# Choosing the engine of squares, sums, residual adds and norm-weight products one by one while a schedule is built

## The reference, cut to what matters

```python
for layer in range(2):
    xn = rmsnorm(h, mix_norm_g[layer])            # h * rsqrt(mean(h*h)) * g
    if layer == 0:                                # 1024 -> 2048 columns
        mix = concat(pool_mixer(a), gate_b * short_conv(gate_c * xb)) @ ab_w_out
    else:                                         # 1024 -> 2560 columns
        uv = gelu(p[..., :1024]); u, v = split(uv)
        c_out = u * (W_s @ layernorm(v) + b)      # in chunks of 128 positions
        # attention of 8 heads: weight = sigmoid(z_ts) * prod_{s<j<t} (1 - sigmoid(z_tj))
        d_out = stick_breaking_attention(q, k, v)
        mix = concat(c_out, d_out) @ cd_w_out
    h = h + mix
    hn = rmsnorm(h, mlp_norm_g[layer])
    h = h + square(relu(hn @ mlp_w1[layer])) @ mlp_w2[layer]      # 1024 -> 4096 -> 1024
return rmsnorm(h, final_norm_g)
```

## Time and profile before

| what | value |
|---|---|
| median of three runs | 2921.53 us (2921.23 to 2926.58) |
| the profiled execution | 2921.85 us |
| its span on the slowest core (core 5) | 2920.1 us; the eight cores 2896.3 to 2920.1 |
| mean granted TensorE clock on core 5 | 0.983 |
| PE, PEld | 2797.7 us (96%), 1194.9 us (41%) |
| DVE, ACT, POOL | 1436.4 (49%), 1261.6 (43%), 1602.0 us (55%) |

### The profile page before, as it was taken

One profiled execution on the slowest core, in us unless ns is written; L12 is line 12 of the kernel. 1 busy time (PEld: TensorE's weight loads), 2 busy tenths in 40 slices (PEclk: granted clock), 3 DMA queues, 4 the chain that ended last, 5 costly groups with the idle time before them and its releaser, 6 DMA issues.

```text
span 2920.1 us, 43942 instructions; the slowest of 8 cores (2896.3 to 2920.1 us)
## 1 busy us (share of the span) xinstructions
PE 2797.7 (96%) x13211; PEld 1194.9 (41%) x13211; DVE 1436.4 (49%) x1759; ACT 1261.6 (43%) x2062; POOL 1602.0 (55%) x1793
## 2 busy tenths in 40 slices
PE   8999999999999999799998999999999989999998
PEld 3444444444443344343443444444444434444443
DVE  4411246464435555776645454445565675554003
ACT  3433234736335344365543353433645464444231
POOL 4655515765417777576761465550576766674333
PEclk9999999999999999899999999999999999999999
DMA  8798883456665999746755344465355485446222
GB/s 171 157 208 196 177 216 90 120 150 147 184 155 107 193 177 175 190 123 157 167 139 155 85 107 113 114 157 170 92 123 123 106 216 135 114 114 184 86 77 83
DMA packets 491478, 420.24 MB, mean 144 GB/s; under 512 B 310128, under 2 KB 334960, under 8 KB 491248
## 3 DMA queue, kind: packets, MB, share of 16 engines
q1 hardware_dynamic: 465184, 370.07, 49.1%
q0 software_dynamic: 26064, 47.36, 11.3%
HBM read 304.23 MB, written 89.13 MB: 135 GB/s over the span
## 4 chain that ended last, share of the span: by engine, by line
PE 79%; DMA 6%; DVE 6%; issue 4%; POOL 3%; ACT 2%; SPq 1%; DVEq 0%; POOLq 0%; ACTq 0%
PE ps L588 74%; PE ps L1349 3%; PE ps L1402 2%; DMA stg<-xT 2%; DMA ring<-wblk 1%; DVE vt L1209 1%; DVE P L1365 1%; DMA h<-xT 1%; POOL Wq L1379 1%; DMA Wk<-Wq 1%; SPq L581 1%; DVE X L746 1%; POOL ps L1064 1%; DMA ring<-wbf 1%; POOL ffB L937 0%
## 5 line engine op out<-in xcount | busy, mean ns | idle before, releaser
L588 PE MATMUL ps<-X,ring 128*128 128x512 bf16 x6144 | 1399.1, 383 | 36.3 <-DVE X L746 11.1
L588 PEld LDWEIGHTS ps<-X,ring 128*128 128x128 bf16 x6144 | 586.0, 98 | 778.9 <-issue 121.5
L1379 POOL TENSOR_TENSOR Wq<-P 128x1024 bf16<-128x1024 f32 (+2 forms) x320 | 529.1, 1655 | 299.3 <-DVE P L1365 289.7
L588 PE MATMUL ps<-mix,ring 128*128 128x512 bf16 x2816 | 657.0, 380 | 7.2 <-POOL P L1360 4.1
L1365 DVE TENSOR_TENSOR_SCAN P<-ps,carry,cbs 128x512 f32<-128x512 f32 x384 | 488.9, 1279 | 346.1 <-POOL P L1360 200.6
L578 ACT ACTIVATE ps<-ps 128x512 f32<-128x512 f32 (+3 forms) x576 | 429.6, 750 | 477.4 <-PE ps L588 238.2
L588 PE MATMUL ps<-ffB,ring 128*128 128x512 bf16 x2048 | 485.1, 380 | 0.0
L811 DVE TENSOR_TENSOR tmp<-ps,ms 128x512 f32<-128x512 f32 x256 | 175.3, 685 | 494.0 <-PE ps L588 493.3
L816 POOL TENSOR_TENSOR h<-tmp,h 128x512 f32<-128x512 f32 x224 | 287.7, 1284 | 229.9 <-DVE tmp L811 229.1
L588 PEld LDWEIGHTS ps<-mix,ring 128*128 128x128 bf16 x2816 | 263.8, 98 | 339.7 <-issue 39.6
L1365 DVE TENSOR_TENSOR_SCAN P<-ps,cbs 128x128 f32<-128x128 f32 (+3 forms) x256 | 208.1, 819 | 323.6 <-ACT ps L578 189.4
(11 more groups left out here) (82 smaller groups left out, 1755.2 us busy)
## 6 DMA issues: line engine op xcount, KB each, us to landing
ring<-wbf SPq DMA_DIRECT2D x540, 256.0 KB, 3.0
ring<-wblk POOLq DMA_DIRECT2D x180, 256.0 KB, 7.9
wbf<-ring SPq DMA_DIRECT2D x180, 256.0 KB, 6.4
stg<-xT SPq DMA_DIRECT2D x96, 256.0 KB, 4.8
h<-xT SPq DMA_DIRECT2D x64, 256.0 KB, 7.4
hsp<-h SPq DMA_DIRECT2D x64, 256.0 KB, 3.7
h<-hsp SPq DMA_DIRECT2D x64, 256.0 KB, 6.2
oT<-mixf SPq DMA_DIRECT2D x32, 256.0 KB, 5.1
```

What stands on the lines that cost most here:

```text
L588: ins = pe.matmul(out, lhsT=l, rhs=r, start=(first and i == 0), stop=(last and i == n - 1), skip_group_check=True)
L1379: yield Req("pool", lambda e: e.tensor_tensor(out=W4, in0=P[:, :, 1:w + 1].rearrange("p h (j n) -> p h j n", n=128), in1=P[:, :, 0:w].rear ...
```

## The change

Three things change. First, a `Req` may carry alternatives: `Machine.run` works out, for each, planned start plus duration plus a cost, and books the one that comes out least. Squares, sums of squares, residual adds and products with the norm weights get alternatives on POOL, ACT or DVE; a MLP tile now always gets a Relu into tmp, and its square any of three engines. Second, planned numbers are replaced, with a price of 1.28 us for a change of ACT's function table. Third, an S stage's out_proj takes the scratch at t = 0, not at t = 1.

```diff
-DMA_KB_US = 256.0
+DMA_KB_US = 230.0
...
+        if r.tab is not None and r.tab != self.tab:
+            self.tab = r.tab
+            start += 1.28
...
                     st = S.ready(r)
+                    if r.alts:
+                        k0 = st + r.dur + r.cost
+                        for q in f.req.alts:
+                            s1 = S.ready(q)
+                            if s1 + q.dur + q.cost < k0:
+                                k0, r, st = s1 + q.dur + q.cost, q, s1
...
+    def any_of(self, *reqs):
+        reqs[0].alts = reqs[1:]
+        return reqs[0]
+
+    def sq_any(self, out, in_, reads, writes, dve=False, bias=0.0):
+
+        p = Req("pool", lambda e: e.tensor_tensor(out=out, in0=in_, in1=in_, op=ALU.mult), reads, writes, 1.06, bias=bias)
+        d = Req("dve", lambda e: e.tensor_tensor(out=out, in0=in_, in1=in_, op=ALU.mult), reads, writes, 0.70, bias=bias)
+        d.cost = 1.5
+        a = Req("act", lambda e: e.activation(out=out, in_=in_, func=AF.Square), reads, writes, 0.63, bias=bias)
+        return self.any_of(p, a, d) if dve else self.any_of(p, a)
...
-        if x == 2 and not odd:
-            yield Req("pool", lambda e: e.tensor_tensor(out=Xf[:, SQ[i][odd], hs], in0=sq, in1=sq, op=ALU.mult), Ls,
-                          [LX[k][t] for k in rows[odd]], 1.15, bias=0.5)
+        if x:
+            yield self.sq_any(Xf[:, SQ[i][odd], hs], sq, Ls, Lw)
...
+            yield self.any_of(add("pool", 1.29, 0.0), add("dve", 0.72, 0.3 if x == 1 and i == 3 or eng == "dve" else 1.5))
...
-            if c % 2:
-                yield Req("dve", lambda e: e.tensor_scalar(out=X[:, c, ts], in0=self.h[:, c, ts], scalar1=g, scalar2=None,
-                                                           op0=ALU.mult),
-                          [self.Lh[c][t], self.Lcf], [LX[c][t]], 0.50)
-            else:
-                yield Req("act", lambda e: e.activation(out=X[:, c, ts], in_=self.h[:, c, ts], func=AF.Copy, scale=g),
-                          [self.Lh[c][t], self.Lcf], [LX[c][t]], 0.72)
+            d = Req("dve", lambda e: e.tensor_scalar(out=X[:, c, ts], in0=self.h[:, c, ts], scalar1=g, scalar2=None,
+                                                     op0=ALU.mult),
+                    [self.Lh[c][t], self.Lcf], [LX[c][t]], 0.55)
+            d.cost = 0.2
+            yield self.any_of(d, Req("act", lambda e: e.activation(out=X[:, c, ts], in_=self.h[:, c, ts], func=AF.Copy, scale=g),
+                                     [self.Lh[c][t], self.Lcf], [LX[c][t]], 0.72))
...
+            yield self.any_of(add("pool", 1.29, 0.0), add("dve", 0.71, 0.2 if last and c >= 6 else 1.5))
...
-                if (j + t) % 2:
-                    b = yield self.p_tmp
-                    m = self.tmp[:, b, :]
-                    yield self.act(m, ap, AF.Relu, [], [self.Lbank[bk], self.Ltmp[b]], TT, True)
-                    self.banks.free(bk)
-                    yield Req("pool", lambda e: e.tensor_tensor(out=F[:, jj, ts], in0=m, in1=m, op=ALU.mult),
-                              [self.Ltmp[b]], [LF[jj][t]], 1.15)
-                    self.p_tmp.free(b)
-                else:
-                    yield self.act(ap, ap, AF.Relu, [], [self.Lbank[bk]], TT, True)
-                    yield self.act(F[:, jj, ts], ap, AF.Square, [], [self.Lbank[bk], LF[jj][t]], TT, True)
-                    self.banks.free(bk)
+                b = yield self.p_tmp
+                m = self.tmp[:, b, :]
+                yield self.act(m, ap, AF.Relu, [], [self.Lbank[bk], self.Ltmp[b]], TT, True)
+                self.banks.free(bk)
+                yield self.sq_any(F[:, jj, ts], m, [self.Ltmp[b]], [LF[jj][t]], True)
+                self.p_tmp.free(b)
...
-            if t == 1:
-                yield lambda: not self.finbusy
+            if t == 1 or kind == "S":
+                yield lambda: not self.finbusy or kind == "S" and t == 0
                 self.use_scratch("ff")
...
-        yield Req("pe", zmm, [self.LqT[a][tq], self.LkT[a][c]], Lz, w / 2400.0 + 0.07, bias=-0.04, wslack=0.5)
+        yield Req("pe", zmm, [self.LqT[a][tq], self.LkT[a][c]], Lz, w / 2400.0 + 0.37, bias=-0.04, wslack=0.5)
...
-                  [LWq], [LWk[r]], 1.25, key=("wk", k, r), lat=4.0, kb=w * 0.69)
+                  [LWq], [LWk[r]], 1.22, key=("wk", k, r), lat=1.6, kb=w * 0.4)
...
-                      0.15 + 0.216 * (2.5 if first else 4), bias=-0.04, slack=4.0)
+                      0.45 + 0.216 * (2.5 if first else 4), bias=-0.04, slack=4.0)
```

More of the change, by code:

```diff
@@ L197 @@
 class Req:
-    __slots__ = ("eng", "fn", "reads", "writes", "key", "dur", "lat", "bias", "kb", "slack", "wslack")
+    __slots__ = ("eng", "fn", "reads", "writes", "key", "dur", "lat", "bias", "kb", "slack", "wslack", "alts", "cost", "tab")
     def __init__(self, eng, fn, reads, writes, dur, key=None, lat=0.0, bias=0.0, kb=256.0, slack=0.0, wslack=0.0):
@@ L211, in __init__ @@
         self.wslack = wslack
+        self.alts = ()
+        self.cost = 0.0
+        self.tab = None
 class Pool:
@@ L698, in square, with add @@
             yield lambda: c - 1 in ev.done
-            if i == 3 and x == 1:
-                eng = "dve"
-            yield Req(eng, lambda e: e.tensor_tensor(
-                out=X[:, SQ[i][2], t * TT:(t + 1) * TT].rearrange("p (a n) -> p a n", a=2),
-                in0=Xf[:, SQ[i][0], hs], in1=Xf[:, SQ[i][1], hs], op=ALU.add),
-                [LX[k][t] for k in rows[1]], [LX[k][t] for k in rows[0]], 0.70 if eng == "dve" else 1.15)
+            def add(eng, d, cost):
+                q = Req(eng, lambda e: e.tensor_tensor(
+                    out=X[:, SQ[i][2], t * TT:(t + 1) * TT].rearrange("p (a n) -> p a n", a=2),
+                    in0=Xf[:, SQ[i][0], hs], in1=Xf[:, SQ[i][1], hs], op=ALU.add),
+                    [LX[k][t] for k in rows[1]], [LX[k][t] for k in rows[0]], d)
+                q.cost = cost
+                return q
+            yield self.any_of(add("pool", 1.29, 0.0), add("dve", 0.72, 0.3 if x == 1 and i == 3 or eng == "dve" else 1.5))
             ev.sums.add(i)
@@ L814, in evac, with add @@
             self.banks.free(bk)
-            eng, d = ("dve", 0.70) if last and c >= 6 else ("pool", 1.15)
-            yield Req(eng, lambda e: e.tensor_tensor(out=self.h[:, c, ts], in0=self.tmp[:, b, :], in1=self.h[:, c, ts],
-                                                     op=ALU.add),
-                      [self.Ltmp[b]], [self.Lh[c][t]], d)
+            def add(eng, d, cost):
+                q = Req(eng, lambda e: e.tensor_tensor(out=self.h[:, c, ts], in0=self.tmp[:, b, :], in1=self.h[:, c, ts],
+                                                       op=ALU.add),
+                        [self.Ltmp[b]], [self.Lh[c][t]], d)
+                q.cost = cost
+                return q
+            yield self.any_of(add("pool", 1.29, 0.0), add("dve", 0.71, 0.2 if last and c >= 6 else 1.5))
             self.p_tmp.free(b)
```

29 lines of the change are left out of this document (17 added, 12 removed).

## The result

The kernel after takes 2959.34 us (median of four runs, 2954.13 to 2964.15); the ratio to the runs of before is 1.0126, 95% interval 1.0105 to 1.0147. It is slower by 1.3%; forecast were 2914.5 us and a range to 2934. For the kernel after it is +39 us, against the 2908.4 to 2909.2 us of the runs of before in the experiments; against the one profiled run of before that was measured with it, it is 36.

A forecast was written before the change was run, and what follows sets the result against it. PE was taken as the bound, busy 2797.7 of 2920.1 us. Terms -7 - 3 + 1.5 + 1 + 1.5 - 1 = -7.0 gave 2914.8 for the profiled run, 2914.5 for the median; range 2896 to 2934.

The forecast's parts named there:

- part 2: F00's W2: new DMA figures spread the x products and remove an old PE wait; -3 us, bounds -5.4 and +8.
- part 5: AV matmuls nearer to their last scores, median distance 88 to 64 matmuls, may wait for transposes; +1.5 us, bounds 0 to +13.
- late transposes: Second form of slower: AV waits in S00 at their upper bound, 2928.5 us; chance 0.07 together with F00.
- Part 1: End of S00's out_proj: PE's 6.23 us wait for POOL's last sum and slow clock behind it shrink; -7.0 us.
- Part 3: Out_projs: 63 more norm-weight products on DVE at 0.835 us overfill it; +1.5 us, bounds 0 to +15; adds cost nothing.
- 0.49 us for a product beside an idle POOL: DVE norm-weight product when POOL is idle; if all 63 were so, their term would be about +0.5 instead of +1.5.
- The 1.26 us product of the earlier trace: A DVE norm-weight product beside POOL, said to end where a POOL sum ends, taken as agreeing with shared SBUF interfaces.
- Part 4: W1 beside attention: MLP squares on ACT add 3.7 us per 20, making 20.8 and 21.6; +1 us, bounds 0 to +5.
- the rival on it: Slower: ACT bounds W1 under attention in six stages; +9.5 us, 2931 us, chance 0.18.
- the 10 that were to show an ACT at its limit: Sign of a wrong forecast: PE waits on ACT ps, ACT tmp or ACT ffB of 10 us and more.
- Part 6: S00's late score: a 4.6 us wait shortens because a POOL square before the scan leaves; -1 us, bounds 0 to -6.
- What stays: Norm chains ending in DVE X, 29.8 us of PE waits, held as long after the change, since all links stay.

The follow-up runs named there:

- e10: Kernel after with only the scores' and AV's planned durations of before, the transposes' new landing kept: ratio 1.0025, +6.8 us.
- e1: Kernel before with one edit, every MLP tile's Relu into tmp and its square on ACT: ratio 0.9988, -4.8 us.
- e9: Kernel after with only the transposes' planned numbers of before, the scores' and AV's longer durations kept: ratio 1.0116, +38.7 us.
- e6: Kernel after with attention's planned numbers of before (scores, AV and transposes): ratio 1.0022, +5.3 us.
- e4: Kernel after with the planned numbers of before and the scratch at t = 1, engine choices kept: ratio 1.0004, -0.2 us.
- e13: Kernel before with a matmul of 512 columns planned at 0.2257 us instead of 0.2157: one run, 2929.1 us, +10.3 us.
- e14: Kernel after with the planned matmul at 0.2057 us instead of 0.2157: ratio 1.0056, +21.2 us.
- e17: Kernel before with attention's new planned numbers and the planned matmul at 0.2057 us: ratio 1.0061, +22.1 us.
- e5: Kernel after with an S stage's out_proj taking the scratch at t = 1 again: ratio 1.0147, two runs, +33 us.
- e7: Kernel after with the planned DMA rate (256) and kept blocks' size (150) of before: ratio 1.0089, +27 us.
- e8: Kernel after without a price for ACT's table switch, Ln 1.3 and Exp 0.9 as before: ratio 1.0091, +30 us.

## Why the prediction was wrong

The step that failed is the list of parts itself. From the new planned numbers the prediction took the DMA figures (part 2) and the transposes' landing (part 5) and priced the places where they move something; the scores' and AV's planned lengths, which the diff shows, have no term. They carry 32 of the 39 us: undone alone, they give that much back (e10). The range ended at 2934 because its upper terms were an ACT at its limit and late transposes. That the time rose and not fell was among the rivals, but for reasons that the runs do not bear out.

- *Part 1, S00's wait*: right in kind. 6.23 became 2.48 us, the slow matmuls behind it are gone; about 5 us instead of 7. S00 as a whole lost 2.9.
- *Part 2, F00*: the wait at its place went, but the loads then stood at the stage's end (12.38 against 2.46 us). F00 came out at +0.7 on the profiled core and +3.6 in the median of the eight, not -3, inside its bounds. That ACT's squares would push the prefetch there (e1) was not seen.
- *Part 3, products on DVE*: +8.8 us of waits on DVE h, not +1.5; with the old lengths +2.6 (e10), so the term was near by itself. A product took 835 ns on average as before. The adds on DVE, costed at nothing, took 1319 ns each, where they had taken 842. Kernel before, then after:

```profile
L816 DVE TENSOR_TENSOR h<-tmp,h 128x512 f32<-128x512 f32 x32 | 27.0, 842 | 3.3
```

```profile
L822 DVE TENSOR_SCALAR X<-h,cfs 128x512 bf16<-128x512 f32 x127 | 106.0, 835 | 14.0 <-DVE h L818 0.5
...
L845 DVE TENSOR_TENSOR h<-tmp,h 128x512 f32<-128x512 f32 x63 | 83.1, 1319 | 6.9 <-DVE tmp L840 0.5
```

  These means hide two lengths, which show when each instruction's time is laid beside POOL's. In the kernel after the 43 products with POOL idle took 485 to 489 ns each, and the 80 with POOL busy for more than half of their time 1039 on average; of the adds, the 21 with POOL idle took 691 to 694 and the 38 with POOL busy 1707 on average. So the prediction's 0.49 us for a product beside an idle POOL holds, but POOL was idle beside only a third of them, even with 334 us less to do. (The 1.26 us product of the earlier trace rows ends 0.3 us behind the POOL sum, at 892.05 against 891.76, not with it.) And the adds' mean rose because 38 of 63 now ran beside POOL, where 7 of 32 had.

- *Part 4, squares on ACT, and the rival on it*: ACT does fill up,

```profile
1320.00:1340.00 20.00, 19.91 (x98) 7.87 (x96) 6.60 (x8) 18.62 (x32) 6.58 (x10) 1.00 0.24 62
2120.00:2140.00 20.00, 20.00 (x95) 8.34 (x93) 10.15 (x8) 18.58 (x30) 7.35 (x9) 1.00 0.35 92
```

  18.6 of 20 us where the estimate had 20.8 to 21.6, and PE waits 4.4 us for tmp and 2.5 for ffB, less than the 10 that were to show an ACT at its limit. The edit alone costs nothing (e1), so ACT was not what bound W1.
- *Part 5, AV*: the waits came (8.6 us, estimate 1.5, bound 13), and were not the loss: taking them away gave nothing back (e9). The nearness I saw in the order was a true sign with the wrong price.
- *Part 6*: the 4.6 us wait is gone, but waits on scans grew from 6.1 to 9.7 us in smaller ones.
- *What stays*: I held the norm chains to be as long as before, since their links stay, and gave pb no term. Waits on DVE X, which end the norm chains, went from 29.8 to 42.8 us and pb from 8.2 to 15.1, because other work stands in front of the links in DVE's queue, at F00's end and at F10's start.

Shown: which numbers do it in the kernel after (e6, e9, e10), and that the engine choices cost nothing by themselves (e4). Argued from the traces and only partly shown: that scores planned too long let the plan put other engines' work in front of what PE soon needs. e13, e14 and e17 give the planned total a part of it, between about an eighth and a half (3 of 26, 10 of 26, 18 of 39); how the rest comes about is open. So is how much of any one run is mere reordering, and so are differences of some 6 us: e5, e7 and e8 lie that close together, for different reasons.
